# Second attention: softmax sums by ones columns beside the values, the sink as a seventeenth meta key, reciprocals no longer spread by matmul

## The chip, the cores and the metric

The kernel runs on one core of a Trainium2 chip. The metric is the device time in microseconds (us) of one execution. Three runs of the kernel before gave 2410.91, 2411.11 and 2414.94 us; the median is 2411.11 us.

## The reference, cut to what matters

Two network blocks follow each other; the change touches only the attention of the second block's last layer, a windowed attention with 32 query heads, 4 shared key/value heads of 64 columns, 16 meta tokens and one learned sink score for each query head. For a query row the weights are

```python
def sink_softmax(sc, sink):
    m = jnp.maximum(jnp.max(sc, axis=-1, keepdims=True), sink)
    e = jnp.exp(sc - m)
    return e / (jnp.sum(e, axis=-1, keepdims=True) + jnp.exp(sink - m))
...
    sr = jnp.einsum('bnqkgd,bnskd->bnkgqs', qr, kb).astype(jnp.float32) * scale
    sr = jnp.where(valid[None, :, None, None, None, :], sr, -jnp.inf)
    pr = sink_softmax(sr, sink[None, None, :, :, None, None])
    orr = jnp.einsum('bnkgqs,bnskd->bnqkgd', pr.astype(v.dtype), vb).reshape(B, S, D_MODEL)
```

The sink takes part in the row maximum and in the sum, and has no value row. Everything is float32.

## The kernel before, in words

One program streams all weights through the core in slabs. A slab is loaded by SP's DMA queue into `raw`. ACT copies it rounded to `whi` (`cast`, L484 to L490), DVE writes the remainder to `wlo` (`lo`, L972 to L976), and PE multiplies with both (`tok_unit` L1620, `gate_unit` L2067). A piece of 256 contraction rows by 512 columns is one unit; `whi` and `wlo` hold four. So the cast of unit t waits until PE has done unit t-4, and PE waits in unit t for the `lo` of t. All engines walk the same written-out list of t; what an engine does for step t beside the unit stands ahead of its `cast`, `lo` or unit of that t, in program order.

In the last layer t runs from 0 to 71: t 0 to 31 are four chunks of 8 units of query projection, t 32 to 63 four chunks of the gate projection, from t 64 on the output projection runs. In between lies the attention, cut into 16 quads. Quad n is four query heads of one block of 128 tokens. Quads with n // 2 even see 144 keys (below: short quads), the others 272 keys (long quads). Quad n begins at t = a = 12 + 3n (`QUAD_AT`), and its steps are

- a, PE (L2057 to L2065): four score matmuls from `qtb` and `kd`, in four PSUM banks; two at a time use different halves of the rows of the array.
- a+4, DVE (L1495 to L1508): scale and mask to `sb_` (L1502), row maxima (L1505), maximum with the sink (L1506), its negative (L1507), sink minus maximum (L1508, which raises `b_max`).
- a+4, ACT (L880 to L886): exp of the sink term (L883), then four exps to `eb_` with their row sums accumulated (L885).
- a+2 on PE (L2032 to L2041): transposes of `eb_` into the banks `TURN_BANK`; PE runs up to four units behind ACT and DVE, so this comes after a+4 of those.
- a+5, DVE (L1509 to L1516): sum plus sink term, and the reciprocal, spread over 64 columns for each head (`rb`).
- a+6, ACT (L887 to L893): copies of the turned weights to `wtb`.
- a+3, PE (L2042 to L2056): the value product. For each block of keys (128, 16 and for long quads 128 more) two matmuls, each with 64 columns of `vb` as weights, give the two halves of bank 3's partitions; then two matmuls turn `rb` into columns 256 to 511 of bank 3.
- a+7, ACT (L894 to L899): copy of the turned reciprocals to `rr`; a+7, DVE (L1517 to L1525): product with `rr` to `ob` (raises `b_o`).

As a+7 of quad n-1 is a+4 of quad n, ACT copies `rr` of quad n-1 behind the exps of quad n, and DVE waits for it before it goes on to `lo`. At t % 8 == 3 ACT's `pair_out` (L901, first half) empties a chunk of the query projection; in the second half DVE's `gb` (L1538) does it, ahead of the quad's work, and ACT's `gate_out` (L912) follows. `gb_silu` and `gb_times` come at t % 8 == 4, `ob_lo` at 7, `rope_q` at 4 and 5 in the first half.

Ahead of the quads `rope_k` (L1482, t = 7) makes the rotated keys `kk`, GpSimd (POOL) copies them to `kd` by four DMAs (L470 to L474), and ACT scales the values into `vb` (L931 to L937). ACT waits for all of `kd` at t = 11 (L941), because `qx` lies over `kk`; the query heads then go through `pair_out`, `rope_q` and a turn on PE (t = 10, L2108).

## Time and profile before

| what | value |
| --- | --- |
| median of 3 runs | 2411.11 us |
| profiled execution, its own time | 2417.06 us |
| span of its trace | 2415.3 us |
| PE, DVE, ACT, POOL busy | 94%, 67%, 47%, 5% |
| mean granted TensorE clock | 0.992 of full speed |
| share of PE in the chain that ended last | 81% |
| units and quads, first scores to last value product | 2072.6 to 2303.0 us |

PE is the engine of matrix products, PEld its weight loads, DVE the vector engine, ACT the scalar engine. A float32 matmul stands as two records, a transpose or a matmul of the rounded type as one. "Idle <- X" behind an instruction means that its engine stood still before it until X was done; "issue" is a wait for nothing that the profile shows. The chain is followed back from the last instruction, always to what released it.

### The profile page before, as it was taken

The numbers are of one execution on the slowest core, as the hardware profiler recorded it, in microseconds if no ns is written. First come the engines' busy times: TensorE is split into PE (matmuls) and PEld (weight loads), VectorE is DVE, ScalarE is ACT, GpSimd is POOL, SyncE is SP. The second block draws the span as 40 slices with busy tenths as digits, with TensorE's granted clock in tenths as the row PEclk, the third lists the DMA queues.
The fourth block names the chain that finished last, engine by engine and source line by source line (L and its number), as shares of the span: only waits on it lengthen the run. The fifth ranks groups of instructions, "written<-read, shape, count | busy, mean of one in ns | idle before, by whom it ended". The sixth has DMA issues, their size and how long they took to land.

```text
span 2415.3 us, 34866 instructions
## 1 busy us (share of the span) xinstructions
PE 2278.3 (94%) x13215; PEld 1980.4 (82%) x13215; DVE 1609.2 (67%) x1948; ACT 1129.1 (47%) x1693; POOL 114.6 (5%) x214
## 2 busy tenths in 40 slices
PE   1399999999989999999999999999999999999897
PEld 1388888887778888888888889999999999778786
DVE  7766677767768875666656776667667546666654
ACT  0255544434355553455445554444544445545443
POOL 0000100011100000000000000000000000000000
PEclk9999999999999999999999999999999999999999
DMA  9888888888957766555555555444444545433353
GB/s 401 321 279 288 271 278 268 260 287 308 322 174 261 246 216 199 172 196 186 193 185 192 194 179 171 158 140 146 136 153 142 162 153 155 146 117 105 105 192 105
DMA packets 219366, 492.92 MB, mean 204 GB/s; under 512 B 9347, under 2 KB 12089, under 8 KB 214105
## 3 DMA queue, kind: packets, MB, share of 16 engines
q1 hardware_dynamic: 195280, 415.27, 50.7%
q0 software_dynamic: 18752, 67.71, 8.7%
q10 hardware_dynamic: 5210, 8.20, 1.0%
q8 instruction: 88, 1.44, 0.2%
q14 instruction: 36, 0.29, 0.0%
HBM read 488.49 MB, written 2.10 MB: 203 GB/s over the span
## 4 chain that ended last, share of the span: by engine, by line
PE 81%; DVE 9%; DMA 5%; issue 3%; ACT 2%; DVEq 0%; POOL 0%; POOLq 0%; SPq 0%; ACTq 0%
PE ps L1629 32%; PE ps L1647 20%; PE ps L1662 13%; PE ps L1664 6%; DMA ada<-in_ada_w 4%; DVE acc L1031 2%; PE ps L2078 2%; DVE wlo L975 1%; DMA rawv<-in_ada_w 1%; PE ps L1905 1%; DVE acc L984 1%; PE ps L2048 1%; PE ps L1679 1%; PE ps L1745 1%; ACT eb__127 L885 1%
## 5 line engine op out<-in xcount | busy, mean ns | idle before, releaser
L975 DVE TENSOR_TENSOR wlo<-raw,whi 128x1024 fp32r<-128x1024 f32 x720 | 873.6, 1222 | 530.9 <-ACT whi L490 529.2
L490 ACT ACTIVATE whi<-raw 128x1024 fp32r<-128x1024 f32 x720 | 756.3, 1057 | 785.2 <-PE ps L1629 421.6
L1662 PE MATMUL ps<-xt__53,whi 128*128 128x512 f32 x1408 | 498.1, 399 | 2.3 <-DVE wlo L975 1.3
L1664 PE MATMUL ps<-xt__53,wlo 128*128 128x256 f32 x1408 | 395.3, 281 | 0.0
L1629 PE MATMUL ps<-whi,xt__53 128*128 128x512 f32 x1024 | 325.8, 395 | 5.0 <-DVE wlo L975 5.0
L1647 PE MATMUL ps<-xmh__54,whi 128*128 128x272 f32 x1088 | 322.5, 296 | 3.9 <-DVE ks L1333 3.3
L1662 PEld LDWEIGHTS ps<-xt__53,whi 128*128 128x128 f32 x1408 | 264.5, 188 | 68.5 <-DVE h L1128 2.2
L1647 PE MATMUL ps<-xmh__54,wlo 128*128 128x272 f32 x1088 | 314.9, 289 | 0.0
L1647 PE MATMUL ps<-xml__55,whi 128*128 128x272 f32 x1088 | 313.0, 288 | 0.0
L1664 PEld LDWEIGHTS ps<-xt__53,wlo 128*128 128x128 f32 x1408 | 266.0, 189 | 0.1
L1629 PEld LDWEIGHTS ps<-whi,xt__53 128*128 128x128 f32 x1024 | 193.4, 189 | 45.3 <-issue 5.5
L1647 PEld LDWEIGHTS ps<-xmh__54,whi 128*128 128x128 f32 x1088 | 205.0, 188 | 11.6 <-issue 10.3
L1647 PEld LDWEIGHTS ps<-xml__55,whi 128*128 128x128 f32 x1088 | 205.1, 189 | 0.5
L1647 PEld LDWEIGHTS ps<-xmh__54,wlo 128*128 128x128 f32 x1088 | 204.8, 188 | 0.0
L1629 PE MATMUL ps<-wlo,xt__53 128*128 128x512 f32 x512 | 200.3, 391 | 0.0
L984 DVE SCALAR_TENSOR_TENSOR acc<-ada,ccol,acc 128x1024 f32<-128x1024 f32 x128 | 163.9, 1280 | 36.9 <-DMA ada<-in_ada_w 36.7
L1629 PE MATMUL ps<-whi,hth 128*128 128x512 f32 x352 | 138.8, 394 | 0.5 <-DVE htl L1209 0.5
L1629 PE MATMUL ps<-whi,htl 128*128 128x512 f32 x352 | 137.2, 390 | 0.0
L1629 PE MATMUL ps<-wlo,hth 128*128 128x512 f32 x352 | 137.0, 389 | 0.0
L1629 PEld LDWEIGHTS ps<-wlo,xt__53 128*128 128x128 f32 x512 | 96.8, 189 | 19.6 <-issue 0.2
L1629 PE MATMUL ps<-whi,ush 128*128 128x512 f32 x256 | 101.1, 395 | 4.0 <-DVE wlo L975 4.0
L413 POOL DMA_DIRECT2D ada<-in_ada_w x128 | 68.1, 532 | 685.7 <-DVE acc L984 670.5
(285 smaller groups left out, 3272.8 us busy)
## 6 DMA issues: line engine op xcount, KB each, us to landing
raw<-in_a_w_in SPq DMA_DIRECT2D x128, 1024.0 KB, 5.5
raw<-in_ffn_w_up SPq DMA_DIRECT2D x88, 1024.0 KB, 5.1
ada<-in_ada_w POOLq DMA_DIRECT2D x128, 512.0 KB, 4.6
raw<-in_a_w_out SPq DMA_DIRECT2D x48, 1024.0 KB, 5.4
raw<-in_ffn_w_down SPq DMA_DIRECT2D x44, 1024.0 KB, 5.1
rawv<-in_ada_w SPq DMA_DIRECT2D x32, 1024.0 KB, 7.2
raw<-in_b_w_in SPq DMA_DIRECT2D x32, 1024.0 KB, 5.3
raw<-in_b_w_out SPq DMA_DIRECT2D x16, 1024.0 KB, 5.2
```

The source lines that it names most:

```text
L413: pool.dma_start(ada[:, half], src).then_inc(al[half], 16)
L490: act.activation(whi[:, r % 4], raw[:, r // 2, r % 2], ACT.Copy).then_inc(hi_ready, 1)
L885: act.activation(eb_[:, i, 0:nk], sb_[:, i, 0:nk], ACT.Exp, bias=st[:, 128 + i:129 + i], accum_out=st[:, 140 + i:141 + i]).then_inc(sem("b ...
L975: dve.tensor_tensor(wlo[:, r % 4], raw[:, r // 2, r % 2], whi[:, r % 4].bitcast(F32), ALU.subtract).then_inc(lo_ready, 1)
L984: dve.scalar_tensor_tensor(out=y, in0=ada[:, half], scalar=ccol[:, bass.ds(kt, 1)], in1=y, op0=ALU.mult, op1=ALU.add).then_inc(ada_step, 1)
L1031: dve.scalar_tensor_tensor(out=acc[:, j], in0=rawv[:, q], scalar=ccol[:, bass.ds(i * 4 + q, 1)], in1=acc[:, j], op0=ALU.mult, op1=ALU.add) ...
L1629: mm = pe.matmul(ps[:, bank + tok, :], xs[x], w[:, r % 4, i, :], start=first and i == 0 and n == 0, stop=last and i == 1 and n == 2)
L1647: mm = pe.matmul(ps[:, bank + c, 0:n_tok], ws[w], x[:, 2 * r + i, 0:n_tok], start=first and i == 0 and n == 0, stop=last and i == 1 and n ...
L1662: pe.matmul(both, whi[:, r % 4, i, c * P:c * P + P], xt_[:, :, k * T:k * T + T], start=first and i == 0, stop=last and i == 1, skip_group_ ...
L1664: mm = pe.matmul(ps[:, bank + c, 0:T], wlo[:, r % 4, i, c * P:c * P + P], xth[:, k, :], start=False, stop=last and i == 1, skip_group_chec ...
L1679: mm = pe.matmul(ps[:, 4 + k % 4, c0:c0 + w], src[0:w, k * P:k * P + P], dg[0:w, d, 0:w], start=True, stop=True)
L2078: mm = pe.matmul(y, ws[w], token_cols(x, (2 * r + i) * L), start=r + c % 2 + i + n == 0, stop=r == 7 and i == 1 and n == 2, skip_group_che ...
```

## The change

The value tile `vb` gets columns of ones between the four heads' values (one, v0, one, v1, one, ...), so that a window of 128 columns holds a head's values in one half and ones in the other. Each of the two products of a key block now uses such a window as weights and fills all 128 partitions of its half of bank 3: output rows in one half, the softmax sum, already spread over 64 partitions, in the other. The sink becomes key 144 (`SINK`): `kd` has a zero column there, DVE copies the sink score over that score, and `vb`'s row for it has zeros for the values and ones for the sum. Gone are the sink's own maximum, difference and exp, the accumulation in ACT's exps, the sum of a+5 and the spread reciprocal, its turn on PE and ACT's copy. New are two reciprocals on DVE at a+7, each on 64 partitions by 256 elements straight from PSUM, and two products in place of one. Bank 3 no longer takes the turned meta keys (bank 7 does), and PE's wait for `b_o` moves from the transposes to the value product. The key DMAs are eight in place of four, and ACT's copy to `vb` waits for `kk_ready`, behind DVE's filling of `vb`.

```diff
-TURN_BANK = (2, 3, 4)
+TURN_BANK = (2, 7, 4)
+BKEYS = ((0, P), (P, NM + 1), (P + NM + 1, P))
+SINK = P + NM
...
-        kd = place("kd", [P, 4, L], O_ACC)
-        vb = place("vb", [P, 3, 256], O_ACC + 4352)
+        kd = place("kd", [P, 4, L + 1], O_ACC)
+        vb = place("vb", [P, 3, 9 * BH], O_ACC + 8 * KB)
...
                 for half in range(2):
-                    pool.dma_start(kd[64 * half:64 * half + 64, e:4:2, :],
-                                   kk[64 * e:64 * e + 64, 0:2, :]).then_inc(sem("kd_ready"), 16)
+                    for c0, c1 in ((0, SINK), (SINK, L)):
+                        g = c0 // SINK
+                        pool.dma_start(kd[64 * half:64 * half + 64, e:4:2, c0 + g:c1 + g],
+                                       kk[64 * e:64 * e + 64, 0:2, c0:c1]).then_inc(sem("kd_ready"), 16)
...
             def quad_act(t):
 
                 for n in quads(t, 4):
-                    nk = (144, L)[n // 2 % 2]
+                    nk = (SINK + 1, L + 1)[n // 2 % 2]
                     act.wait_ge(sem("b_max"), n + 1)
-                    act.activation(st[:, 136:140], st[:, 132:136], ACT.Exp).then_inc(sem("b_sexp"), 1)
                     for i in range(4):
-                        act.activation(eb_[:, i, 0:nk], sb_[:, i, 0:nk], ACT.Exp, bias=st[:, 128 + i:129 + i],
-                                       accum_out=st[:, 140 + i:141 + i]).then_inc(sem("b_exp"), 1)
+                        act.activation(eb_[:, i, 0:nk], sb_[:, i, 0:nk], ACT.Exp, bias=st[:, 128 + i:129 + i])\
+                           .then_inc(sem("b_exp"), 1)
...
-                for n in quads(t, 7):
-                    act.wait_ge(sem("b_pv"), n + 1)
-                    if n:
-                        act.wait_ge(sem("b_o"), n)
-                    act.activation(rr[:, :, :], ps[:, 3, 256:512].rearrange("p (k q) -> p k q", q=P),
-                                   ACT.Copy).then_inc(sem("rr_ready"), 1)
...
                     act.wait_ge(sem("vb_turned"), 1)
+                    act.wait_ge(sem("kk_ready"), 1)
                     for b, (c0, w) in enumerate(BLK):
                         bank, col = ((1, 0), (1, 256), (0, 0))[b]
                         r = B_SCALE[b]
-                        cp = act.activation(vb[0:w, b, :], ps[0:w, bank, col:col + 256], ACT.Copy, scale=st[0:w, r:r + 1])
+                        dst = vb[0:w, b, BH:9 * BH].rearrange("p (j x d) -> p j x d", x=2, d=BH)[:, :, 0, :]
+                        cp = act.activation(dst, ps[0:w, bank, col:col + 256].rearrange("p (j d) -> p j d", d=BH), ACT.Copy,
+                                            scale=st[0:w, r:r + 1])
                     cp.then_inc(sem("vb_ready"), 1)
...
-                        act.wait_ge(sem("kd_ready"), 64)
+                        act.wait_ge(sem("kd_ready"), 128)
...
+                dve.memset(kd[:, :, SINK:SINK + 1], 0.0)
+                own4(dve.memset(vb[:, :, :], 1.0))
+                dve.memset(vb[0:NM + 1, 1, BH:9 * BH].rearrange("p (j x d) -> p j x d", x=2, d=BH)[:, :, 0, :], 0.0)
                 dve.tensor_tensor(kk[:, 0:2, :], kt1[:, :, :], kt2[:, :, :], ALU.add).then_inc(sem("kk_ready"), 1)
...
-                    own6 = Own(dve, sem("quad_own"), n * 6)
-                    nk = (144, L)[tok]
+                    own6 = Own(dve, sem("quad_own"), n * 3)
+                    nk = (SINK + 1, L + 1)[tok]
+                    if n:
+                        dve.wait_ge(sem("b_exp"), 4 * n)
                     dve.wait_ge(sem("b_scores"), n + 1)
-                    s = sb_[:, :, 0:nk]
+                    x = sb_[:, :, 0:nk]
                     sink = sinkb[:, j * 8 + 4 * half:j * 8 + 4 * half + 4]
-                    own6(dve.scalar_tensor_tensor(out=s, in0=ps[:, 4:8, 0:nk], scalar=BH ** -0.5,
+                    own6(dve.scalar_tensor_tensor(out=x, in0=ps[:, 4:8, 0:nk], scalar=BH ** -0.5,
                                                   in1=maskB[:, tok:tok + 1, 0:nk].broadcast_to([P, 4, nk]),
                                                   op0=ALU.mult, op1=ALU.add))
-                    own6(dve.tensor_reduce(st[:, 120:124], s, AX.X, ALU.max))
-                    own6(dve.tensor_tensor(st[:, 124:128], st[:, 120:124], sink, ALU.max))
-                    own6(dve.tensor_scalar(st[:, 128:132], st[:, 124:128], -1.0, None, ALU.mult))
-                    dve.tensor_tensor(st[:, 132:136], sink, st[:, 124:128], ALU.subtract).then_inc(sem("b_max"), 1)
-                for n in quads(t, 5):
-                    own6 = Own(dve, sem("quad_own"), n * 6 + 4)
-                    dve.wait_ge(sem("b_sexp"), n + 1)
-                    dve.wait_ge(sem("b_exp"), n * 4 + 4)
-                    own6(dve.tensor_tensor(st[:, 144:148], st[:, 140:144], st[:, 136:140], ALU.add))
-                    if n:
-                        dve.wait_ge(sem("b_o"), n)
-                    own6(dve.reciprocal(rb[:, :, :], st[:, 144:148].unsqueeze(2).broadcast_to([P, 4, BH])))
+                    own6(dve.tensor_copy(sb_[:, :, SINK:SINK + 1], sink.unsqueeze(2)))
+                    own6(dve.tensor_reduce(st[:, 120:124], x, AX.X, ALU.max))
+                    dve.tensor_scalar(st[:, 128:132], st[:, 120:124], -1.0, None, ALU.mult).then_inc(sem("b_max"), 1)
                 for n in quads(t, 7):
                     j, tok, half = n // 4, n // 2 % 2, n % 2
                     dve.wait_ge(sem("b_pv"), n + 1)
                     k = 4 * j + 2 * half
-                    dve.wait_ge(sem("rr_ready"), n + 1)
-                    dve.tensor_tensor(ob[:, k:k + 2, tok * P:tok * P + P],
-                                      ps[:, 3, 0:256].rearrange("p (k q) -> p k q", q=P),
-                                      rr[:, :, :], ALU.mult)\
-                       .then_inc(sem("b_o"), 1)
+                    for e in range(2):
+                        if n:
+                            dve.wait_ge(sem("b_o"), 2 * n - 1 + e)
+                        o0, s0, c0 = e * BH, (1 - e) * BH, e * T
+                        r = rr[o0:o0 + BH, :, :]
+                        dve.reciprocal(r, ps[s0:s0 + BH, 3, c0:c0 + T].rearrange("p (k q) -> p k q", q=P))\
+                           .then_inc(sem("rr_ready"), 1)
+                    for e in range(2):
+                        o0, c0 = e * BH, e * T
+                        dve.wait_ge(sem("rr_ready"), 2 * n + e + 1)
+                        dve.tensor_tensor(ob[o0:o0 + BH, k:k + 2, tok * P:tok * P + P],
+                                          ps[o0:o0 + BH, 3, c0:c0 + T].rearrange("p (k q) -> p k q", q=P),
+                                          rr[o0:o0 + BH, :, :], ALU.mult).then_inc(sem("b_o"), 1)
...
-                    for kb in (0, 2, 1) if tok else (0, 1):
-                        kc, w = BLK[kb]
-                        if n and kb == 1:
-                            pe.wait_ge(sem("b_o"), n)
+                    for kb in range(2 + tok):
+                        kc, w = BKEYS[kb]
                         for i in range(4):
                             mm = pe.transpose(ps[0:w, TURN_BANK[kb], i * P:i * P + P], eb_[:, i, kc:kc + w], ident[:, :])
                     mm.then_inc(sem("b_wturned"), 1)
                 for n in quads(t, 3):
                     j, tok = n // 4, n // 2 % 2
                     pe.wait_ge(sem("b_wt"), n + 1)
+                    if n:
+                        pe.wait_ge(sem("b_o"), 2 * n)
                     for kb in range(2 + tok):
-                        w = BLK[kb][1]
+                        w = BKEYS[kb][1]
                         for e in range(2):
-                            mm = pe.matmul(ps[e * BH:e * BH + BH, 3, 0:256], vb[0:w, kb, j * BH:j * BH + BH],
-                                           wtb[0:w, kb, e:4:2, :], start=kb == 0, stop=kb == 1 + tok,
+                            c0 = (2 * j + 1 - e) * BH
+                            mm = pe.matmul(ps[:, 3, e * T:e * T + T], vb[0:w, kb, c0:c0 + 2 * BH],
+                                           wtb[0:w, kb, e:4:2, :], start=kb + e == 0, stop=kb == 1 + tok,
                                            skip_group_check=True)
-                    pe.wait_ge(sem("quad_own"), n * 6 + 6)
-                    for k in range(2):
-                        mm = pe.matmul(ps[:, 3, 256 + k * P:256 + k * P + P],
-                                       rb[:, 2 * k:2 * k + 2, :].rearrange("p e d -> p (e d)"), ident[:, :],
-                                       start=True, stop=True, skip_group_check=True)
                     mm.then_inc(sem("b_pv"), 1)
```

## Rows read from the trace of the kernel before

**Rows 1.** Table by stretches, all 16 quads: length, busy us (instructions) of each engine.

```profile
2066.00:2306.00 240.00, 225.51 (x1507) 181.99 (x1508) 157.66 (x221) 120.07 (x275) 0.00 (x0) 0.96 0.36 113
```

**Rows 2.** Timeline of PE: start, us, instruction, idle before it and its releaser.

```profile
2066.08 1.06 PE L2087 MATMUL ps<-ident,qx 128*128 128x128 f32 x8 [0.78 <-DVE qx L1536]
...
2105.02 1.53 PE L2040 MATMUL ps<-ident,eb__127 128*128 128x128 f32 x12 [1.32 <-ACT eb__127 L885]
...
2125.79 3.20 PE L2048 MATMUL ps<-wtb,vb 128*64 128x256 f32 x12 [2.20 <-ACT wtb L891]
...
2204.90 1.40 PE L2040 MATMUL ps<-ident,eb__127 128*128 128x128 f32 x8 [1.83 <-ACT eb__127 L885]
...
2242.55 3.22 PE L2048 MATMUL ps<-wtb,vb 128*64 128x256 f32 x12 [4.50 <-ACT wtb L891]
...
2283.32 0.35 PE L2078 MATMUL ps<-xmh__54,whi 128*128 128x256 f32 x1 [1.54 <-DVE gb L1547]
```

**Rows 3.** Table by stretches, PE alone, behind its two longest stops; then granted clock.

```profile
2126.00:2132.50 6.50, 6.50 (x27) 0.50 0.53 175
2242.50:2251.50 9.00, 8.95 (x40) 0.50 0.35 117
```

**Rows 4.** Chain that ended last, quads 0 and 2: start, us, what.

```profile
2082.91 1.16 PE ps L2048 x8
...
2110.21 1.74 PE ps L2048 x12
2111.95 0.64 PE ps L2053 x4
```

**Rows 5.** The same view in other stages: float32 products of 256 columns, full array width.

```profile
308.98 1.73 PE ps L1745 x8
```

```profile
1619.09 1.69 PE ps L1905 x6
```

**Rows 6.** Groups of DVE by line in the quads: count, busy us, mean ns.

```profile
L1516 DVE RECIPROCAL rb<-st 128x256 f32<-128x256 f32 x16 | 28.0, 1753 | 0.6
```

**Rows 7.** Timeline of DVE, quad 14, a long one.

```profile
2274.62 1.29 DVE L1502 SCALAR_TENSOR_TENSOR sb__126<-ps,maskB 128x1088 f32<-128x1088 f32 x1 [0.61 <-PE ps L2063]
...
2277.27 0.16 DVE L1506 TENSOR_TENSOR st<-st,sinkb 128x4 f32<-128x4 f32 x1
...
2280.47 0.42 DVE L1522 TENSOR_TENSOR ob<-ps,rr 128x256 f32<-128x256 f32 x1 [2.63 <-ACT rr L898]
2281.34 1.23 DVE L975 TENSOR_TENSOR wlo<-raw,whi 128x1024 fp32r<-128x1024 f32 x1 [0.45 <-ACT whi L490]
2282.49 1.28 DVE L1547 TENSOR_TENSOR gb<-ps,rb_b 128x512 f32<-128x512 f32 x2
```

**Rows 8.** Timeline of ACT, quad 14.

```profile
2277.87 0.20 ACT L883 ACTIVATE st<-st 128x4 f32<-128x4 f32 x1 [5.12 <-DVE st L1508]
2277.98 0.51 ACT L885 ACTIVATE eb__127<-sb__126,st 128x272 f32<-128x272 f32 x1
2278.39 0.19 ACT L885 ACTIVATION_READ_ACCUMULATOR eb__127<-sb__126,st 128x1 f32 x1
2278.48 0.51 ACT L885 ACTIVATE eb__127<-sb__126,st 128x272 f32<-128x272 f32 x1
```

**Rows 9.** Waits of PE's weight loads: us in total, times, longest.

```profile
PEld ps L2040 <- DVE ob L1522: 0.7, 2, 0.4
```

**Rows 10.** Tile `kd`: ns min/median/max, first and last start, and time to landing.

```profile
L473 POOL DMA_DIRECT2D kd<-kk x4: 593/597/716, 2049.1 to 2050.9; - x4
...
DMA to landing us min/median/max: 2.4/3.5/6.7
```

**Rows 11.** Tile `maskB`: a fill of 544 columns by DVE.

```profile
L1469 DVE MEMSET maskB<- x1: 512/512/512, 1996.3 to 1996.3; 128x544 f32 x1
```

**Rows 12.** Timeline of DVE and ACT ahead of the quads.

```profile
2048.04 0.72 DVE L1488 TENSOR_TENSOR kk<-kt,kt 128x544 f32<-128x544 f32 x1
```

```profile
2058.46 0.69 ACT L909 ACTIVATE qx<-ps,st 128x512 f32<-128x512 f32 x1 [0.33 <-PE ps L1629]
```

19 lines of the change are left out of this document (9 added, 10 removed).

## Prediction

> **What bounds the kernel now.** The chain on the page runs through PE for most of the span, so I looked for the stretch that the change touches and asked how near PE is to its limit there. In the 240 us of the quads PE is busy 225.5 us, PEld 182, DVE 157.7, ACT 120 [rows 1]. What PE loses stands in its timeline: six stops of over 0.4 us that matter here, 0.78, 1.32, 2.20, 1.83, 4.50 and 1.54 us [rows 2], together 12.2. Two of them are followed by a stretch at the lower clock level, 6.5 and 9 us at a granted 0.50, that is 1.2 GHz [rows 3]. At half speed these cost about half their length, 3.3 and 4.5 us. The reader is to see that the engine is full between the stops: work added to PE costs its own length, while work taken from DVE and ACT pays only where a stop ends on it.
>
> **Part 1, the value product on PE.** Before, a short quad's product takes 1.16 us and a long one's 1.74, that is 0.58 for each key block of four records, and the turn of the reciprocals 0.64 [rows 4]: 1.80 and 2.38. The two halves of a block lie in different column halves of the array; afterwards each fills the full width. The nearest rows for that are eight records in 1.73 us, 0.216 each, where the number of contraction rows stays, and six in 1.69, where it goes from 128 to 16 and back [rows 5]; 6 x 0.216 = 1.30, so each change of rows costs 0.20. A long quad (128, 17, 128 rows) becomes 12 x 0.216 + 2 x 0.20 = 2.99, so +0.61. A short one becomes 8 x 0.216 + 0.20 = 1.93 and some 0.13 where it leaves 17 rows for the scores: 2.06, so +0.26. Eight of each: 8 x 0.87 = +7.0 us. Without any cost of changed rows it would be 8 x (0.21 - 0.07) = +1.1; with 0.20 at every border of a block, three to a quad for long ones and two and the exit for short ones, +10.6. I take 7.0, since the row with changing rows is the same operation. The scores gain one column in 144 or 272 and the transposes one row: nothing.
>
> The skill has a rule that speaks against this part. The Trainium skill, TensorEngine Tiling (Array Packing), Performance Considerations, has a weight tile of at most 64 columns run as two tiles with up to twice the rate, and its Key Properties say that "changing tiling mode (not just tile) drains the TensorE". By the first taken in full, giving the packing up doubles 1.16 and 1.74, and the part would cost about +13; the rows bear out a ratio of 1.5 without and 1.8 with a change of rows (0.58 against 0.86 and 1.06 for a block), not two.
>
> **Part 2, the way from scores to exps.** DVE loses two small operations and gains one copy, each 0.16 and its gap [rows 7]: 0.2 sooner. ACT loses the sink exp, 0.11 ahead of the first exp, and four accumulator reads of 0.09 (2278.39 to 2278.48) [rows 8]: 0.47. So `b_exp`, for which PE's transposes wait, comes 0.7 us sooner, and the copy of `rr` behind it is gone.
>
> **Part 3, DVE's tail.** Before, DVE stands 2.63 us for `rr` in a long quad (2.2 in a short one), multiplies in 0.42 [rows 7], and at a+5 spends 0.16 + 1.75 on sum and reciprocal [rows 6]: 4.6 to 5.0 us a quad. Afterwards it waits for nothing, since the product of quad n-1 stands ahead of the scores of quad n on PE, and spends two reciprocals and two products. No row shows a reciprocal from PSUM on 64 partitions. Its bounds are 0.9 (half, if partitions counted) and 2.1 (a fifth more for PSUM); I take 1.75, as the fills and products here go by elements in a partition. 3.5 + 0.04 + 2 x 0.38 = 4.3 us. In sum 0.3 to 0.7 less, but differently placed. In a long quad the first `lo` began 6.7 us after the mask (2274.62 to 2281.34) [rows 7]; now 1.29 + 0.03 + 0.19 + 1.32 + 0.17 + 4.3 = 7.3, 0.6 later, in a short one 1.0 later. The `lo` after it comes 1.3 or 0.9 sooner. What is queued behind the new work is `lo`, and `gb` or `rope_q` where they fall in that t. PE needs that `lo` four units (11 us) after the scores: hidden, except behind `gb`.
>
> **Part 4, the stops, one by one.** 1.32 at quad 2: the mask began 1.7 us after the scores because DVE came late from reciprocal and rope. It now comes at the scores' end, and the exps 0.7 sooner: the stop goes, -1.3. 2.20 at quad 3: ACT's `pair_out` waits for the unit that PE has just done, then 1.4 us of `wtb` copies. Nothing of this changes; it and its slow stretch stay. Quads 9 to 11: the 1.83 falls to 1.1, the wait for bank 3 inside the transposes (0.4 of [rows 9]) goes, DVE reaches the masks of quads 10 and 11 0.9 and 1.8 sooner, and `gb` ahead of the 4.50 starts 2.5 to 3 sooner. Walking the three engines through it I get the product of quad 11 3.0 us sooner although 0.9 of part 1 lies ahead, so -3.9 and a stop of about 3.1, which I take to be followed by the slow stretch as before. The other bank wait, at quad 1: -0.3. PE's new wait for `b_o` ahead of the product: DVE is done with quad n-1 some 7.5 us after the scores, PE comes at 9: no cost. 1.54 at 2283.32: unit 56 waits for `gb`, which stands behind quad 14's work and that `lo` [rows 7]: +0.6 and a stop of 2.1.
>
> **Part 5, ahead of the quads.** `rope_k` gets a fill of 3 x 576 = 1728 columns (0.51 for 544 [rows 11], so 1.6 by proportion) and two small ones: `kk` is ready 2.0 us later, at 2050.8 for 2048.76 [rows 12]. ACT's values (three copies, 1.2), cast 7 (1.05) and `lo` 7 (1.23) now follow one another behind it and end at about 2054.4; PE comes to unit 7 at 2056.7, half a unit ahead of the 2058.1 at which ACT's first `pair_out` is released [rows 12]: hidden, with 2 us to spare. POOL's eight DMAs of 0.6 each [rows 10] begin at 2051.0; the last at 2055.3, landing 2.4 to 6.7 us later, 2057.7 to 2062.0, middle 2059.8. ACT used it at 2058.46 [rows 12], and up to 2059.2 nothing behind is late; then the turn of the queries, which already stops PE for 0.78, is late by as much. I take +0.6, between 0 and 2.8.
>
> **Sum.** 7.0 + 0.6 + 0.6 - 1.3 - 3.9 - 0.3 = +2.7 us. The profiled execution took 2417.06 us with a span of 2415.3; by the sum its like would take 2419.8. The median of the runs is 5.95 us lower, and I set the difference on the median: 2413.8.
>
> **The rivals.** *The clock falls once more.* Stops of 1.83 us and less left the clock alone, those of 2.20 and 4.50 did not [rows 2, 3]. The stop at unit 56 goes to 2.1, the one at the queries' turn to 1.4 and with late DMAs up to 3.6. From about 2 us it decides: a slow stretch of 6.5 to 9 us costs 3.3 to 4.5, so 2417.7, or 2420 with the DMAs late. Against it: both estimates lie just under. *The product costs its upper bound,* 10.6: 2417.4. By the skill's factor of two, 13, it would be near 2420. *DVE becomes the bound.* If a reciprocal from PSUM costs its 2.1 and my walk is out elsewhere, DVE's 1.8 us more busy time a quad show in the eight quads beside the gate: 14 us, 2428. Against it: DVE is at 158 of 240 us and its idle wait for `rr` pays for it. *Faster.* The product costs its lower bound (-5.9: 2407.9), and the stop of quad 11 shrinks below 2 us without a slow stretch (another -4.5): 2403.4.
>
> **How the numbers follow.** 0.2% is 4.8 us, about what a measurement of this kernel can tell from no change. The forecast, 2409 to 2415.9: 0.49. Clock: 0.19. Product at its bound: 0.09. DVE bound: 0.06. Faster, 2402 to 2406: 0.17. So slower 0.34, same 0.49, faster 0.17. The range of 2404 to 2420 leaves out the DVE case and the outer edges of the clock case and of the faster one, together under 0.2.
>
> **What would show it.** The new product of 8 and 12 records in 2.06 and 2.99 us; 32 reciprocals of 1.75; exps with 0.1 less from start to start; no stop at quad 2, one of 3.1 at quad 11, one of 2.1 at unit 56; the last `kd` DMA landing near 2060; the same two slow stretches and no third. I am wrong if the product costs no change of rows, if a third slow stretch shows, or if DVE's masks begin long after the scores.

## The result, and the profile after

The kernel after took 2422.78 us (median of five runs, 2421.32 to 2424.32), the kernel before beside it 2412.11 us: 1.0041 times as long, 95% interval 1.0029 to 1.0052. A second comparison gave 2421.84 us and 1.0029 (1.0017 to 1.0040). By these ratios it is slower by 7 to 10 us, a little above the 0.2% that can be told apart; the medians themselves lie 10.7 and 6.4 us apart (the ratios are not those of the two medians). The forecast was 2413.8 us with a range of 2404 to 2420, so the time lies above the range.

The kernel before showed a spread that three runs had hidden: in later comparisons its medians were 2414.8 to 2415.7 us, with single runs from 2407 to 2421. Its profiled execution (2417.06 us) was one of the longer ones, the profiled one of after (2421.32 us) one of the shorter. The two traces therefore differ by 4.3 us of span, less than the medians do. Both kernels have a second trace, and I read the four together.

Span and busy time on the page of the kernel after:

```profile
span 2419.6 us, 34617 instructions
...
PE 2283.8 (94%) x13151; PEld 1993.2 (82%) x13151; DVE 1641.2 (68%) x1951; ACT 1116.9 (46%) x1597; POOL 116.5 (5%) x218
```

The same work, from the first scores to the start of unit 64, in the table by stretches (window, length, busy us and instructions of PE, PEld, DVE, ACT, POOL, granted clock, DMA share, GB/s). Before:

```profile
2072.65:2314.73 242.08, 227.36 (x1546) 184.97 (x1545) 159.64 (x224) 120.78 (x274) 0.00 (x0) 0.96 0.35 112
```

Before, profiled again:

```profile
2073.00:2311.45 238.45, 225.22 (x1545) 184.30 (x1545) 159.46 (x224) 120.78 (x274) 0.00 (x0) 0.97 0.36 114
```

After:

```profile
2075.51:2318.97 243.46, 231.76 (x1481) 196.06 (x1481) 190.76 (x224) 109.55 (x178) 0.00 (x0) 0.97 0.35 112
```

The kernel after, profiled again, took 243.49 us there with PE busy 231.73, the same within 0.03. PE is busy 4.4 to 6.5 us more and idle 1.5 to 3.0 us less (11.7 after, 14.7 and 13.2 before). The stretch is 1.4 us longer against the first trace of before and 5.0 against the second. The rest stands ahead of the first scores, which begin at 2075.51 for 2072.65. The traces do not run in step there: DVE's `lo` of t = 5, which is the same work in both and lies ahead of the keys, starts at 2041.38 before and already at 2040.58 after. Counted from it the first scores come 3.7 us later in this trace and 2.2 in the second one of the kernel after; unit 64 comes 3.6 to 8.7 us later, depending on which two of the four traces are compared, 6.2 in the mean.

PE's stops in the timeline of the kernel after (start, us, instruction, idle before it and its releaser), to be read against [rows 2] and against a stop of the kernel before that neither [rows 2] nor the prediction has, at quad 10:

```profile
2219.47 1.53 PE L2040 MATMUL ps<-ident,eb__127 128*128 128x128 f32 x12 [1.49 <-ACT eb__127 L885]
```

After:

```profile
2067.37 1.94 PE L2086 MATMUL ps<-ident,qx 128*128 128x128 f32 x8 [2.87 <-DVE qx L1539]
...
2127.55 5.13 PE L2052 MATMUL ps<-wtb,vb 128*128 128x256 f32 x12 [2.20 <-ACT wtb L893]
...
2207.96 1.09 PE L2041 MATMUL ps<-ident,eb__127 128*128 128x128 f32 x8 [1.17 <-ACT eb__127 L887]
...
2221.92 1.53 PE L2041 MATMUL ps<-ident,eb__127 128*128 128x128 f32 x12 [1.11 <-ACT eb__127 L887]
...
2244.39 5.87 PE L2052 MATMUL ps<-wtb,vb 128*128 128x256 f32 x12 [3.79 <-ACT wtb L893]
...
2286.19 0.35 PE L2077 MATMUL ps<-xmh__54,whi 128*128 128x256 f32 x1 [2.54 <-DVE gb L1550]
```

The stop at quad 2 (1.32) is gone, the 2.20 is as it was, 1.83 became 1.17, 1.49 became 1.11 and 4.50 became 3.79. Two stops grew: 0.78 to 2.87 at the queries' turn, and 1.54 to 2.54 at unit 56. The product behind the 2.20 takes 5.13 us for 3.20.

The value products where the clock is full, in the chain of the kernel after (start, us, what), the counterpart of [rows 4]:

```profile
2085.60 1.92 PE ps L2052 x8
...
2111.43 2.98 PE ps L2052 x12
```

And the chain just ahead of the queries' turn, for which [rows 12] give the times of before:

```profile
2047.27 0.06 DVE kd L1487
...
2047.64 1.51 DVE vb L1488
...
2049.24 0.27 DVE vb L1489
2049.51 0.59 DVE kk L1490
2050.10 0.28 issue
2050.39 0.71 POOL kd L476
2051.10 3.47 POOL kd L476 x6
2054.57 6.06 DMA kd<-kk
2060.63 0.02 issue
2060.66 1.13 ACT qx L905 x2
```

The chain shows the whole way: 2.2 us of fills and their gaps ahead of `kk`, eight DMA issues, and the last of them landing 6.06 us after its issue. ACT's `pair_out` starts on that landing, at 2060.66 for 2058.46 before (3.0 us later, counted from the `lo` of t = 5), and the turn of the queries follows from it.

### The profile page after: what moved, and what is told of

It is laid out like the page before. It is cut to its first block, busy times and chain, and to the rows that moved or that the text cites. A ratio compares the mean times of both kernels' runs of the same rounds, so it can differ in the third digit from the quotient of the medians.

```text
span 2419.6 us, 34617 instructions
## 1 busy us (share of the span) xinstructions
PE 2283.8 (94%) x13151; PEld 1993.2 (82%) x13151; DVE 1641.2 (68%) x1951; ACT 1116.9 (46%) x1597; POOL 116.5 (5%) x218
## 4 chain that ended last, share of the span: by engine, by line
PE 83%; DVE 8%; DMA 4%; issue 2%; ACT 1%; POOL 0%; DVEq 0%; POOLq 0%; SPq 0%; ACTq 0%
PE ps L1632 33%; PE ps L1650 20%; PE ps L1665 13%; PE ps L1667 6%; DMA ada<-in_ada_w 3%; PE ps L2077 3%; DVE acc L1030 2%; PE ps L2052 2%; DVE wlo L974 1%; DMA rawv<-in_ada_w 1%; PE ps L1908 1%; DVE acc L983 1%; PE ps L2062 1%; PE ps L2041 1%; PE ps L1682 1%
```

## The experiments

All ratios are to runs of the kernel before on the same chip, taken beside those of the edited kernel; differences in us are these ratios times 2415. One part in a thousand is 2.4 us.

**The kernel before, once more.** No edit.

> The kernel before, unchanged, for its spread and a second trace. The change measured +10 us on the medians, but only +4.3 us between the two profiled executions, whose before took 2417.06 us against a median of 2412.1. Theory A (the executions of before differ in how many stretches at half clock they have): the trace shows a time near 2411 with one of the two slow stretches of the first trace (behind the stops at the products of quads 3 and 11) missing or shorter, 3 to 5 us less between 2126 and 2252. Theory B (the difference lies in loading and the early stages): both slow stretches are there and the time is lost or won before 2000 us.

Measured: 2415.54 us, 1.0005 (0.9996 to 1.0014). Its stops are those of [rows 2]: 0.78, 1.33, 2.20, 1.83, 4.50, 1.53; the 1.49 at quad 10 is missing. And behind the same 2.20 it has no slow stretch:

```profile
2126.18 1.81 PE L2048 MATMUL ps<-wtb,vb 128*64 128x256 f32 x12 [2.20 <-ACT wtb L891]
...
2127.92 0.71 PE L2053 MATMUL ps<-ident,rb 128*128 128x128 f32 x4
```

In the table by stretches (columns as above):

```profile
2127.00:2134.00 7.00, 7.00 (x41) 5.14 (x38) 3.52 (x7) 2.52 (x12) 0.00 (x0) 1.00 0.49 150
```

The first profile had a granted 0.50 there [rows 3] and 3.20 us for that product. Instead the lower level follows the stop of 1.83 at quad 9, which left the clock alone in the first trace:

```profile
2203.00:2208.00 5.00, 4.97 (x30) 4.79 (x32) 4.47 (x6) 2.29 (x4) 0.00 (x0) 0.66 0.37 100
```

PE comes later to quad 10 by that and no longer waits there. From the first scores to unit 64 this trace is 3.6 us shorter than the first, with the same code. Of the eleven traces in this document that have the stop of 2.20, nine have the lower level behind it and two (this one and the one with early fills) full clock. So neither the length of a stop nor a single trace settles where a slow stretch falls.

**The kernel after, once more.** No edit.

> The changed kernel, unchanged, beside the others of this call. Before ranged from 2408.7 to 2418.8 us in 35 executions, so the +10 of the first comparison (5 executions each) may be some us off. From the parts so far, late key DMAs +4.3 (before with that part alone) and the quads, where the trace has the product 5.8 us dearer (8 x 0.12 + 8 x 0.60) and the stops 3.4 us shorter: +6.7, with more or fewer slow stretches on top: 7 to 10 us over before.

Measured: 2421.84 us, 1.0029 (1.0017 to 1.0040), span 2420.6. The stops are 2.98 at the queries' turn, then 2.20, 1.17, 1.11, 3.84, 2.54. In the first profile of after the queries' turn ran slow (1.94 us, clock 0.72 in 2066 to 2072); here it took 1.06 us at full clock behind an even longer stop:

```profile
2069.94 1.06 PE L2086 MATMUL ps<-ident,qx 128*128 128x128 f32 x8 [2.98 <-DVE qx L1539]
```

The two executions take 2421.32 and 2422.29 us. So a third slow stretch is not what makes the kernel slower. Taking for each stretch of 10 us from 2060 to 2320 its length times the share of the clock not granted, and adding them up, gives 8.5 and 6.9 us in the two traces of before, and 8.5 and 6.9 in the two of after.

**Part 5 alone: the late key DMAs on the kernel before.**

```diff
+        fill = place("fill", [P, 1988], O_V + 24 * KB)
...
-                    pool.dma_start(kd[64 * half:64 * half + 64, e:4:2, :],
-                                   kk[64 * e:64 * e + 64, 0:2, :]).then_inc(sem("kd_ready"), 16)
+                    for c0, c1 in ((0, 144), (144, L)):
+                        pool.dma_start(kd[64 * half:64 * half + 64, e:4:2, c0:c1],
+                                       kk[64 * e:64 * e + 64, 0:2, c0:c1]).then_inc(sem("kd_ready"), 16)
...
+                    act.wait_ge(sem("kk_ready"), 1)
...
+                dve.memset(fill[:, 0:4], 0.0)
+                own4(dve.memset(fill[:, 4:1732], 1.0))
+                dve.memset(fill[0:NM + 1, 1732:1988], 0.0)
```

> The kernel before with only what the change puts ahead of the quads: the key DMAs in eight parts, three fills of the same size (into unused memory) ahead of the last step of the key rotation, and ACT's values behind that step. If this part carries the loss that I had put at 0.6 us: a stop of 2.5 to 3 us at the queries' turn with a slow stretch, first scores 3 to 4 us later, 2415 to 2416 against 2412. If the loss lies in the quads: within 1 us of before.

Measured: 2419.58 us, 1.0018 (1.0009 to 1.0027), that is +4.3 us (2.2 to 6.5). Its timeline has the one new stop, and its tile `kd` (ns min/median/max, first and last start; then time to landing) the late landing:

```profile
2067.65 1.06 PE L2093 MATMUL ps<-ident,qx 128*128 128x128 f32 x8 [2.84 <-DVE qx L1542]
```

```profile
L475 POOL DMA_DIRECT2D kd<-kk x8: 592/594/714, 2050.7 to 2054.9; - x8
...
DMA to landing us min/median/max: 2.0/2.0/6.0
```

All its other stops are those of before, and from the first scores to unit 64 it takes 242.2 us for 242.1. This part by itself costs the 2 us of that stop, and by the ratio 2.2 to 6.5.

**The change with its fills one step earlier.**

```diff
-                dve.memset(kd[:, :, SINK:SINK + 1], 0.0)
-                own4(dve.memset(vb[:, :, :], 1.0))
-                dve.memset(vb[0:NM + 1, 1, BH:9 * BH].rearrange("p (j x d) -> p j x d", x=2, d=BH)[:, :, 0, :], 0.0)
                 dve.tensor_tensor(kk[:, 0:2, :], kt1[:, :, :], kt2[:, :, :], ALU.add).then_inc(sem("kk_ready"), 1)
...
+                if t == 6:
+                    dve.memset(kd[:, :, SINK:SINK + 1], 0.0)
+                    own4(dve.memset(vb[:, :, :], 1.0))
+                    dve.memset(vb[0:NM + 1, 1, BH:9 * BH].rearrange("p (j x d) -> p j x d", x=2, d=BH)[:, :, 0, :], 0.0)
                 if t == 7:
                     rope_k()
```

> The changed kernel with its three fills of kd and vb moved from the last step of the key rotation (t = 7) one step ahead (t = 6), where DVE stands idle for over 1 us. Nothing else differs. Theory A (late key DMAs): the keys are ready about 1.5 to 2 us sooner, the last of eight DMAs lands near 2059 in place of 2060.7, the stop at the queries' turn falls from 2.87 to about 1 us and the slow stretch behind it goes: 2 to 4 us faster than the changed kernel, 2419 to 2421. Theory B (the eight DMAs are slow by themselves, since the last waits behind a slab): the landing moves by under 0.5 us and the time stays at 2422.8.

Measured: 2419.11 us, 1.0021 (1.0010 to 1.0031); the stop at the queries' turn is 1.51 for 2.87, and all others stay. Against the two results of after, 0.8 to 2.0 parts in a thousand come back, 2 to 5 us, with intervals that overlap (1.0010 to 1.0031 beside 1.0017 to 1.0040 and 1.0029 to 1.0052); the trace shows 1.4 of it. Some 0.7 us of the stop stay against the kernel before. Two things are left that can make it: counted from the `lo` of t = 5, `kk` is still ready 0.8 us later than before (2.1 in the change), as the fills do not fit whole into DVE's pause, and four more issues of 0.6 us stand ahead of the last DMA. No run parts them.

**What the early copy of `rr` and the sink column bring alone.** First only `rr` ahead of the exps on ACT:

```diff
             def quad_act(t):
+                for n in quads(t, 7):
+                    act.wait_ge(sem("b_pv"), n + 1)
+                    if n:
+                        act.wait_ge(sem("b_o"), n)
+                    act.activation(rr[:, :, :], ps[:, 3, 256:512].rearrange("p (k q) -> p k q", q=P),
+                                   ACT.Copy).then_inc(sem("rr_ready"), 1)
                 for n in quads(t, 4):
...
-                for n in quads(t, 7):
```

> The kernel before with one order changed: ACT copies the turned reciprocals of quad n-1 ahead of the exps of quad n in place of behind them, so DVE's product no longer waits for the exps (2.63 us a long quad, 2.2 a short one). It gives DVE the relief that the change gives, without its cost on PE. Theory A (stops end on DVE's tail): the stops of 1.32 at quad 2 and 1.54 at unit 56 go, that of 4.50 falls to about 3: 3 to 6 us faster than before, 2406 to 2409. Rival (the exps start 0.3 later where the copy stands ahead of them, and the stops are structural): within 1 us of before.

Measured: 2412.53 us, 0.9990 (0.9981 to 0.9999), 2.4 us and less than I expected. The stops at quads 2, 9 and 10 stay (1.42, 1.83, 1.53), since they hang on the exps. Only the later two shrink: 4.50 to 4.24, 1.54 to 1.27. Then the sink as one more column of `sb_` on top of it, with bank 7 for the meta keys and the product as it was:

```diff
-TURN_BANK = (2, 3, 4)
+TURN_BANK = (2, 7, 4)
...
-                    act.activation(st[:, 136:140], st[:, 132:136], ACT.Exp).then_inc(sem("b_sexp"), 1)
                     for i in range(4):
-                        act.activation(eb_[:, i, 0:nk], sb_[:, i, 0:nk], ACT.Exp, bias=st[:, 128 + i:129 + i],
+                        act.activation(eb_[:, i, 0:nk + 1], sb_[:, i, 0:nk + 1], ACT.Exp, bias=st[:, 128 + i:129 + i],
                                        accum_out=st[:, 140 + i:141 + i]).then_inc(sem("b_exp"), 1)
...
+                    own6(dve.tensor_copy(sb_[:, :, nk:nk + 1], sink.unsqueeze(2)))
+                    dve.wait_ge(sem("b_scores"), n + 1)
...
-                    own6(dve.reciprocal(rb[:, :, :], st[:, 144:148].unsqueeze(2).broadcast_to([P, 4, BH])))
+                    own6(dve.reciprocal(rb[:, :, :], st[:, 140:144].unsqueeze(2).broadcast_to([P, 4, BH])))
```

> From the kernel before with the copy of the reciprocals ahead of the exps: the sink is written as one more column behind the scores in sb_ (not a key: no column in kd, no row in vb), so the row maximum and the accumulated sums take it in; sink maximum, difference, sink exp and the sum of a+5 go; bank 7 in place of 3 takes the turned meta keys. Packed product and spread reciprocals stay. It has the change's relief on DVE and ACT without its product and its late keys. Theory (product and key DMAs are what makes the change slow): b_exp 0.5 us sooner, the 1.32 stop at quad 2 gone, 1.83 to 1.3, 4.50 to about 3, unit 56's near 1: 4 to 7 us faster than before. Rival (the relief is worth nothing since the stops are structural): within 2 us.

Measured: 2409.40 us, 0.9982 (0.9969 to 0.9994). Stops 0.89, 2.20, 1.55, 1.09, 3.95 and 0.85. The sink as a column, with `rr` early, is the good half of the change: the stop at unit 56 halves instead of growing, and no ones columns are needed for it. The exps still accumulate their sums here, so what leaving the accumulator reads out is worth was not tried alone; the stops at quads 2 and 9 are 0.89 and 1.55 with them, none and 1.17 in the change.

**The change with one reciprocal in place of two.** It leaves out that half of the heads are divided by their own sums.

```diff
-                    for e in range(2):
-                        if n:
-                            dve.wait_ge(sem("b_o"), 2 * n - 1 + e)
-                        o0, s0, c0 = e * BH, (1 - e) * BH, e * T
-                        r = rr[o0:o0 + BH, :, :]
-                        dve.reciprocal(r, ps[s0:s0 + BH, 3, c0:c0 + T].rearrange("p (k q) -> p k q", q=P))\
-                           .then_inc(sem("rr_ready"), 1)
+                    if n:
+                        dve.wait_ge(sem("b_o"), 2 * n)
+                    dve.reciprocal(rr[:, :, :], ps[:, 3, 0:T].rearrange("p (k q) -> p k q", q=P))\
+                       .then_inc(sem("rr_ready"), 2)
```

> The changed kernel with one reciprocal of 128 partitions by 256 elements in place of two of 64 by 256. It leaves out that half of the heads are divided by their own sums; everything else runs as in the changed kernel. Theory A (DVE's tail of two reciprocals ends the stops at the products of quads 11 and at unit 56): one instruction costs 1.75 whatever the partitions, the stops of 2.54 at unit 56 and 3.79 at quad 11 fall by 1 to 1.8 us each, 2 to 5 us faster than the changed kernel. Rival (PE's dearer product is all that counts): within 1 us of it. Rival 2 (64 partitions cost half of 128): no change of DVE's time at all, same as the changed kernel.

Measured: 2419.68 us, 1.0015 (1.0003 to 1.0027), beside 1.0029 for after. The stops that hang on DVE's tail fall:

```profile
2245.53 6.08 PE L2049 MATMUL ps<-wtb,vb 128*128 128x256 f32 x12 [2.87 <-ACT wtb L893]
...
2286.91 0.35 PE L2074 MATMUL ps<-xmh__54,whi 128*128 128x256 f32 x1 [0.81 <-DVE gb L1547]
```

From 3.84 to 2.87 and from 2.54 to 0.81, together 2.7 us, and the 1.11 at quad 10 goes too. The stretch from first scores to unit 64 is 240.7 us for 243.5: the trace (2.8 us, with 1.7 more of the clock not granted) and the ratios (0.0014, 3.4 us) agree. The intervals of the two ratios overlap, so the size rests on the trace.

**The wide product alone, on the kernel before.** It leaves out that the heads are kept apart: both products of a block use 128 columns of `vb` as weights.

```diff
-                            mm = pe.matmul(ps[e * BH:e * BH + BH, 3, 0:256], vb[0:w, kb, j * BH:j * BH + BH],
-                                           wtb[0:w, kb, e:4:2, :], start=kb == 0, stop=kb == 1 + tok,
+                            mm = pe.matmul(ps[:, 3, 0:256], vb[0:w, kb, j // 2 * P:j // 2 * P + P],
+                                           wtb[0:w, kb, e:4:2, :], start=kb + e == 0, stop=kb == 1 + tok,
```

> The kernel before with its value product alone made wide: 128 columns of vb as weights, all 128 partitions of bank 3's first half, both halves of the heads summed there. It leaves out that the heads are kept apart; the turned reciprocals, ACT and DVE run as before. A short product goes from 1.16 to 1.92, a long one from 1.74 to 2.98: 8 x 0.76 + 8 x 1.24 = 16 us more on PE. If work on PE costs its length here: 13 to 16 us over before (1.0054 to 1.0066). If the stops take it up, since PE waits anyhow: under 8 us.

Measured: 2430.92 us, 1.0074 (1.0060 to 1.0089), +18 us (the medians lie 15.2 apart). The chain has the product at full clock:

```profile
2078.96 1.92 PE ps L2048 x8
...
2107.05 2.98 PE ps L2048 x12
```

Against 1.16 and 1.74 [rows 4] that is 8 x 0.76 + 8 x 1.24 = 16.0 us; the long quads behind the two long stops run it at the lower clock, 5.5 and 6.08 us for 3.2 each, which is another 2.7. From the first scores to unit 64 it takes 256.5 us for 242.1 and 238.4, so 14.4 to 18.1 more, with PE busy 17.1 to 19.3 more and idle 1.2 to 2.7 less; the stop at quad 2 falls from 1.32 to 0.62. PE has little to hide this work behind, and nearly all of it arrives. In the change 10.2 us of it are paid back by the turns of the reciprocals (16 x 0.64), which leaves 5.8.

**The change with values and ones as packed pairs.** On the kernel with early fills: four products of 64 weight columns for each block, values in bank 3's first half, ones in its second, so that one reciprocal and one product on 128 partitions do. The diff shows PE's part alone.

```diff
...
-                        for e in range(2):
-                            c0 = (2 * j + 1 - e) * BH
-                            mm = pe.matmul(ps[:, 3, e * T:e * T + T], vb[0:w, kb, c0:c0 + 2 * BH],
-                                           wtb[0:w, kb, e:4:2, :], start=kb + e == 0, stop=kb == 1 + tok,
-                                           skip_group_check=True)
+                        for ones_too in range(2):
+                            for e in range(2):
+                                c0 = (2 * j + 1 - ones_too) * BH
+                                mm = pe.matmul(ps[e * BH:e * BH + BH, 3, ones_too * T:ones_too * T + T],
+                                               vb[0:w, kb, c0:c0 + BH], wtb[0:w, kb, e:4:2, :],
+                                               start=kb + ones_too == 0, stop=kb == 1 + tok, skip_group_check=True)
```

> The changed kernel with its fills one step ahead, and with values and ones as separate weights of 64 columns, so that the two halves of a block are packed side by side again and a block takes two such pairs; one reciprocal of 128 by 256 and one product on DVE follow. All results are whole. PE: 2 x 0.58 a block, 2.3 a short and 3.5 a long quad in place of 1.92 and 2.98: 7 us more in sum. DVE: 2.2 us less a quad, which took 1 us off the stop at quad 11 and 1.7 off unit 56. Theory (PE pays its length, DVE only at the stops): 3 to 5 us slower than the changed kernel with early fills (1.0021 of before), 1.0035 to 1.005. Rival (pairs share the array so well that a block of two pairs takes no longer than 1.06): 2 to 3 us faster than it.

Measured: 2414.26 us, 0.9993 (0.9983 to 1.0003). The product, in the chain:

```profile
2081.21 2.02 PE ps L2049 x16
...
2107.17 3.04 PE ps L2049 x24
```

I had put 2.3 and 3.5 and a slower kernel. Twice the matmuls take only 0.10 and 0.06 us more than the wide ones: for 16 records 2.02 us, where one after another they would take 3.5 at the 0.216 of a full-width record. DVE is freed (155.3 us busy in the stretch for 190.8), and the stops are 2.88 for 3.85 at quad 11 and 0.70 for 2.53 at unit 56. Against the wide product with the same early fills the two ratios differ by 0.0028, 6.8 us, and their intervals do not touch, but they come from two chips; the two traces differ by only 0.8 us from first scores to unit 64 (241.0 for 241.9: PE idle 3.6 less and busy 2.7 more, with 1.7 more of the clock not granted). So that it is faster is shown, the 6.8 is not. With early fills and packed pairs the change as a whole costs nothing that can be told from zero.

**ACT's `wtb` copies ahead of `pair_out` and `gate_out`.** The two long stops are in both kernels. ACT's timeline of the kernel after at quad 3 shows what stands ahead of the copies:

```profile
2124.07 0.69 ACT L905 ACTIVATE qx<-ps,st 128x512 f32<-128x512 f32 x1 [1.65 <-PE ps L1632]
2125.39 0.69 ACT L905 ACTIVATE qx<-ps,st 128x512 f32<-128x512 f32 x1 [0.64 <-PE ps L1632]
2125.98 1.52 ACT L893 ACTIVATE wtb<-ps 128x512 f32<-128x512 f32 x3
```

The copies wait behind `pair_out`, which waits for the unit that PE has just done. With them moved ahead of it, on the kernel before:

```diff
+            def quad_wtb(t):
+                for n in quads(t, 6):
+                    act.wait_ge(sem("b_wturned"), n + 1)
...
+                    cp.then_inc(sem("b_wt"), 1)
...
+                quad_wtb(t)
                 if t % 8 == 3 and t > 8:
                     n = t // 8 - 1
```

> The kernel before with one order changed: ACT's copies of the turned weights (a+6) stand ahead of pair_out and gate_out where both fall in one t (quads 3 and 11), in place of behind them. The stops of 2.20 at quad 3 and 4.50 at quad 11 end on that order, if it was read right: both go, and with them the slow stretches that mostly follow: 7 to 11 us faster than before. Rival (unit 24 and unit 48 then wait as long for the emptied banks): the stop moves one step down and the gain is under 2 us.

Measured: 2403.09 us, 0.9958 (0.9943 to 0.9973). The 2.20 and the 4.50 are gone (one of 0.84 shows at the turn of quad 11's reciprocals), and with them both slow stretches (columns as above):

```profile
2120.00:2133.00 13.00, 13.00 (x74) 9.51 (x73) 8.90 (x15) 8.04 (x19) 0.00 (x0) 1.00 0.34 99
2236.00:2250.00 14.00, 13.67 (x112) 11.63 (x110) 9.95 (x15) 7.86 (x18) 0.00 (x0) 1.00 0.47 150
```

The clock not granted in 2060 to 2320 falls to 1.7 us, from 6.9 and 8.5; what is left follows the stop of 1.83 (0.72 granted in 2203 to 2209). The same edit on the change with early fills:

> The changed kernel with its fills one step ahead and with ACT's copies of the turned weights ahead of pair_out and gate_out. Without the two long stops PE is almost never idle in the quads, so the dearer product shows in full. Against the same reordering of the kernel before (0.9958 of before): theory (PE's product costs its length, 5.8 us, plus 0.8 of the turn and 1 more at unit 56): 6 to 8 us over it, 2409 to 2411. Rival (DVE's relief makes up for the product): within 2 us of it, 2403 to 2405.

Measured: 2404.82 us, 0.9964 (0.9951 to 0.9977). So against the same edit on before the change costs 0.0006, about 1.5 us, with overlapping intervals, where I had expected 6 to 8; the rival of that expectation held. In the stretch from first scores to unit 64 it is 231.4 us for 229.6, with PE busy 4.2 us more and idle 2.4 less, and 1.7 us of the clock not granted in both. Without the long stops the relief on ACT and DVE pays most of what PE does more.

**Both that paid, together.** The sink as a column with `rr` first, and `wtb` first, on the kernel before.

> The two edits that helped put together: the kernel before with the sink as a column behind the scores, the early copy of the reciprocals and bank 7 (0.18% faster alone), and ACT's copies of the turned weights ahead of pair_out and gate_out (0.42% alone). If the stops are separate, the gains add: 0.55 to 0.65% under before, 2400 to 2402; the stops of quads 3 and 11 gone, quads 9 and 10 near 1.5 and 1.1, unit 56 near 0.85. If one stop only moves into the other: 2403, no better than the reordering alone.

Measured: 2398.22 us, 0.9935 (0.9921 to 0.9948): 15.7 us faster than before, the fastest of all, and nothing is left out. 0.0018 and 0.0042 had been measured apart, so the gains add. Stops 0.78, 0.89, 1.55, 1.09 and 0.85, and no slow stretch:

```profile
2073.30:2297.27 223.97, 218.80 (x1546) 180.66 (x1545) 152.73 (x192) 120.73 (x258) 0.00 (x0) 1.00 0.38 121
```

The packed product together with `wtb` first was not tried.

## Why the prediction was wrong, point by point

**Part 1, the product: right in mechanism, a little high at full clock, and without its slow stretches.** 7.0 expected, 5.8 measured at full clock: 1.92 and 2.98 us in place of 1.80 and 2.38. The long quads came as worked out (2.99). The short ones cost nothing for leaving 17 rows; the 0.13 that I added there was not in any row. The ratio to before is 1.7, a block in 0.96 to 0.99 us for 0.58. The Trainium skill, TensorEngine Tiling (Array Packing), Theoretical Speedup, puts what packing of two tiles gains at up to 2; the measured 1.65 to 1.71 stays under that. The packed experiment shows it from the other side: with packing kept, values and ones take 2.02 us for 1.92.

What the prediction put at nothing is that two of the wide products fall into slow stretches (5.13 and 5.87 us). From first scores to unit 64 all products and turns add up to 46.7 us after, for 39.6 and 37.7 in the two traces of before: 7.2 and 9.1 more. Counted in the same way the pair without long stops (`wtb` first) has 41.9 for 35.7, 6.2 more. So 1.0 to 2.9 us of the loss are the dearer product at the lower level.

**Part 2, the exps: right.** At quad 14 the exps end 4.8 us after the start of the mask, for 5.5 before (I had 0.7 less). The stop at quad 2 went, and quads 9 and 10 stop for 1.17 and 1.11 us, where I had put 1.1 for the first. The exps of quad 14 stand in ACT's timeline as one row of 1.77 us for four; before, each was followed by its read [rows 8].

**Part 3, DVE's tail: right within 0.2.** 4.48 us for 4.3. In DVE's timeline of the kernel after, quad 14, the counterpart of [rows 7]:

```profile
2276.55 1.30 DVE L1506 SCALAR_TENSOR_TENSOR sb__126<-ps,maskB 128x1092 f32<-128x1092 f32 x1 [0.81 <-PE ps L2062]
...
2279.61 3.54 DVE L1521 RECIPROCAL rr<-ps 64x256 f32<-64x256 f32 x2
2283.19 0.88 DVE L1526 TENSOR_TENSOR ob<-ps,rr 64x256 f32<-64x256 f32 x2
2284.09 1.23 DVE L974 TENSOR_TENSOR wlo<-raw,whi 128x1024 fp32r<-128x1024 f32 x1
2285.35 1.29 DVE L1550 TENSOR_TENSOR gb<-ps,rb_b 128x512 f32<-128x512 f32 x2
```

**Part 4, the stops: the first step that failed, in size.** For quads 9 to 11 I had walked the three engines and got the product of quad 11 3.0 us sooner, though 0.9 of part 1 lies ahead (-3.9), and a stop of 3.1 there. Counted from the mask of quad 9 it came 1.9 sooner (39.8 us for 41.7), with 1.0 of part 1 ahead, so -2.9, and the stop was 3.79. The three stops fell from 1.83 + 1.49 + 4.50 = 7.82 to 1.17 + 1.11 + 3.79 = 6.07, which is 1.75. The place where the walk went wrong stands in DVE's timeline at quad 11. Before:

```profile
2228.15 1.28 DVE L1502 SCALAR_TENSOR_TENSOR sb__126<-ps,maskB 128x1088 f32<-128x1088 f32 x1
...
2236.19 1.75 DVE L1516 RECIPROCAL rb<-st 128x256 f32<-128x256 f32 x1
...
2239.12 1.28 DVE L1547 TENSOR_TENSOR gb<-ps,rb_b 128x512 f32<-128x512 f32 x2
```

After:

```profile
2231.03 1.30 DVE L1506 SCALAR_TENSOR_TENSOR sb__126<-ps,maskB 128x1092 f32<-128x1092 f32 x1 [1.82 <-PE ps L2062]
...
2240.96 1.29 DVE L1550 TENSOR_TENSOR gb<-ps,rb_b 128x512 f32<-128x512 f32 x2
```

DVE was early, as I had reckoned, but it then stood 1.82 us for the scores, which PE reaches behind the dearer products of quads 9 and 10. So the mask of quad 11 came 0.8 us sooner after that of quad 9 and not 1.8, and `gb` 1.9 and not 2.5 to 3. From that mask to `gb` the tail is 1.0 us shorter (9.9 for 11.0), since the old spread reciprocal also stood ahead of `gb` there.

At unit 56 I had +0.6 and it was +1.0 (2.54 for 1.54): from the mask to the release of unit 56 now take 9.6 us for 8.7 [rows 2, 7]. Here the old reciprocal came behind `gb` and both new ones stand ahead of it. The experiment with one reciprocal gives back 1.0 us at quad 11 and 1.7 at unit 56: both stops still hang on DVE's tail, through `gb` and, at quad 11, ACT's `gate_out` and `wtb`. By the sum the quads should have cost +2.1; against the second trace of before, whose clock was granted alike (0.97), they cost +5.0: 6.5 more on PE, 1.5 less idle.

**Part 5, the keys: the second step that failed.** I had 2.0 us of delay, the last landing at 2059.8 and a cost of 0.6. The delay was near (2.1, counted from the `lo` of t = 5) and the landing came at 2060.63, which in step with the trace of before is 2061.4, inside my bounds of 2057.7 to 2062.0. The mistake was the middle. ACT waits for the last of eight transfers, so the longest landing counts, not the mean; the trace of before had it, 6.7 for a median of 3.5 [rows 10], and I took the middle of the two ends. With the long end the stop would have come out at 3.6; it was 2.87. The first scores came 2.2 us later, and 3.7 in the execution whose turn ran slow, where I had 0.6: 1.6 and 3.1 us more than predicted. That ACT's values and unit 7 would be hidden was right; PE has no stop there.

**The base.** I had set the sum on the median of three runs, 2411.11 us. Over 17 to 35 runs it lies near 2415, and beside the first runs of after it was 2412.11. So of the miss of 8 to 9 us one comes from the base in the first comparison and some 4 in the second, and not from the change. As a difference I had forecast 2.7 us and it was 7 to 10, so the mechanism was missed by more than the base. The upper end of the range stood 8.9 us above that base, which would have held the smaller of the two differences and not the larger; the range had no term for the base being off.

**The rivals.** *The clock falls once more* was nearest in time (2420 with late DMAs) and wrong in cause: the lower level behind the queries' turn showed in one of two profiles of after, with the same medians, and the clock not granted is the same in both kernels. Its premise, a stop of about 2 us that decides, doesn't hold either: 2.20 was followed by full clock in two traces, 2.84 and 2.98 at the queries' turn too, and 1.83 by the lower level in the second trace of before and in that with `wtb` first. *The product at its upper bound* fell with 5.8. *DVE becomes the bound* is half true: DVE is busy 31 us more in the quads, 1.95 a quad (I had 1.8), but PE waits for it in two places, not in eight quads. One reciprocal less gives 3 us, and one reciprocal and one product less (the packed experiment) 0.8 by the traces and 7 by the ratios, not 14. *Faster* fell.

**What stays open.** Put together at full clock, what was measured is 5.8 for the product, -1.3 and -0.3 for quads 2 and 1 as forecast, -2.9 for quads 9 to 11, +1.0 at unit 56 and +2.2 for the keys: +4.5. With 1.0 to 2.9 for the product in slow stretches it is 5.5 to 7.4, beside 6.2 by the four traces and 7 to 10 by the ratios. The rest is no wider than the intervals, and I can't place it. The -0.3 at quad 1 was not measured apart.

Why the change costs 5.0 us in the quads beside the long stops and only 1.8 without them is settled in part. Of the 3.2 us between them 2.9 are the two long products at the lower level (9.1 more for products and turns there, 6.2 here). But the trace of before that gives the 5.0 has its slow stretches in other places than the kernel after, and against the first trace the quads cost only 1.4. With slow stretches that move from one execution to the next, one trace of each kernel does not give the cost of a stretch to better than some 3 us.

## What to carry to other kernels

Where one engine is full, look at what a simplification puts on it and at the few places where its stops end, rather than at the sum of work saved elsewhere: here five small steps on ACT and DVE went, and one wider matmul and one more reciprocal paid for them. When a wait is for several transfers, cost it by the longest landing in the trace. Put the copy that the bounding engine waits for ahead of copies that nobody needs yet; that one move gained 10 us, as much as the whole change cost, and taking from the change only its cheap half (the sink as a column, with `rr` ahead of the exps) gained another 4 to 6.

## What the runs showed of the hardware

- The lower clock level behind a given stop is not certain. The same 2.20 us stop was followed by a product of 3.20 us in one execution and of 1.81 in another, the same 1.83 us stop by full clock in one and by 0.66 over 5 us in another; stops of 2.84, 2.96 and 2.98 us at the queries' turn by full clock, one of 2.87 by 0.72 over 6 us.
- A reciprocal of 256 elements in a partition takes 1.76 us on 64 partitions from PSUM, 1.76 on 128 from PSUM (one reciprocal) and 1.75 on 128 from SBUF [rows 6]. Halving the partitions halves nothing, and PSUM costs nothing more.
- Float32 products of 256 columns packed two by two in the column halves take 2.02 us for 16 records, against 1.92 for 8 of the full width.
- Of the eight small GpSimd DMAs to `kd` the median landed 2.0 to 2.1 us after its issue and the slowest 6.0 to 6.2, in each of the traces that have eight; of the four in the two traces of the kernel before, 3.3 to 3.5 and 6.5 to 6.7.
